# Softmax weights turned through VectorE and HBM in the attention and convolution layers of an encoder trunk

## The reference

```python
# differential attention: two softmaxes per head, one weight matrix w
probs = jax.nn.softmax(logits, axis=-1)
w = (probs[:, 0] - lam * probs[:, 1]).astype(v.dtype)
return jnp.einsum('bhqk,bkhe->bqhe', w, v)

# memory attention, in every layer
logits = jnp.einsum('bshd,bmhd->bhsm', q, km)
probs = jax.nn.softmax(logits, axis=-1)
return jnp.einsum('bhsm,bmhd->bshd', probs, vm)
```

## Time and profile before

| | |
|---|---|
| device time, median of 3 | 1245.73 us |
| span of the profiled execution, first to last instruction | 1244.68 us |
| what lies around the span, against the median | 1.05 us |
| PE busy | 1235.2 us, 99% |
| DVE busy | 1024.4 us, 82% |
| ACT busy | 730.3 us, 59% |
| mean granted TensorE clock | 0.998 |
| DMA queue of SP | 228.02 MB, 55.5% of 16 engines |

### The profile page before, as it was taken

How to read it: one execution, slowest core, us unless ns; L and a number is a source line. 1 busy time by engine, 2 the same in 40 slices (tenths; PEclk the granted TensorE clock), 3 DMA queues, 4 the chain that set the end, 5 groups by cost and what they waited for, 6 DMA issues and landing times.

```text
span 1244.7 us, 19689 instructions
## 1 busy us (share of the span) xinstructions
PE 1235.2 (99%) x7370; PEld 1082.9 (87%) x7370; DVE 1024.4 (82%) x1599; ACT 730.3 (59%) x1190; POOL 20.1 (2%) x29
## 2 busy tenths in 40 slices
PE   9999999999999999999999999999999999999997
PEld 7988888888999988888889888888888888888886
DVE  5876888889779888988887978988888776988887
ACT  6675765555766546555555546655554774755552
POOL 0001000000000100000000000000000001000000
PEclk9999999999999999999999999999999999999999
DMA  9834576554553345655655764656554533666651
GB/s 333 285 120 136 190 248 190 186 192 163 175 182 119 122 150 169 227 187 195 201 173 168 233 204 162 227 195 199 190 186 169 187 119 119 218 207 201 196 190 54
DMA packets 64539, 229.27 MB, mean 184 GB/s; under 512 B 7575, under 2 KB 9239, under 8 KB 63421
## 3 DMA queue, kind: packets, MB, share of 16 engines
q1 hardware_dynamic: 64444, 228.02, 55.5%
HBM read 226.93 MB, written 1.06 MB: 183 GB/s over the span
## 4 chain that ended last, share of the span: by engine, by line
PE 97%; DMA 1%; SPq 1%; DVE 0%; issue 0%; ACT 0%; DVEq 0%
PE pair L768 28%; PE acc L862 21%; PE pair L771 14%; PE pair L800 4%; PE pair L801 4%; PE pair L802 4%; PE acc L768 2%; PE acc L843 2%; PE acc L842 2%; PE acc L841 2%; PE pair L1022 2%; DMA raw<-in_stream 1%; PE pair L825 1%; PE pair L827 1%; PE pair L829 1%; PE acc L931 1%
## 5 line engine op out<-in xcount | busy, mean ns | idle before, releaser
L1278 DVE TENSOR_TENSOR w_lo<-raw,w_hi 128x1024 fp32r<-128x1024 f32 x400 | 482.6, 1221 | 105.3 <-ACT w_hi L1040 103.7
L1040 ACT ACTIVATE w_hi<-raw 128x1024 fp32r<-128x1024 f32 x400 | 420.5, 1058 | 213.2 <-PE pair L771 70.8
L768 PE MATMUL pair<-xT,w_hi 128*128 128x512 f32 x1520 | 477.8, 396 | 0.0
L771 PEld LDWEIGHTS pair<-xT,w_lo 128*128 128x128 f32 x1520 | 285.5, 188 | 67.2
L771 PE MATMUL pair<-xT,w_lo 128*128 128x256 f32 x1520 | 298.6, 278 | 0.0
L768 PEld LDWEIGHTS pair<-xT,w_hi 128*128 128x128 f32 x1520 | 233.8, 189 | 3.2 <-issue 0.3
L1087 ACT ACTIVATE hid<-pair 128x512 f32<-128x512 f32 x88 | 52.6, 597 | 124.9 <-PE pair L771 124.9
L1319 DVE TENSOR_TENSOR hid<-pair,hid 128x512 f32<-128x512 f32 x88 | 60.7, 690 | 47.9 <-ACT hid L1087 47.7
L800 PE MATMUL pair<-xT,w_hi 128*128 128x256 f32 x336 | 97.8, 291 | 0.0
L801 PE MATMUL pair<-xT,w_hi 128*128 128x256 f32 x336 | 95.0, 283 | 0.0
L802 PE MATMUL pair<-xT,w_lo 128*128 128x256 f32 x336 | 94.9, 283 | 0.0
(11 more groups left out here) (223 smaller groups left out, 1661.9 us busy)
## 6 DMA issues: line engine op xcount, KB each, us to landing
raw<-in_stream SPq DMA_DIRECT2D x400, 512.0 KB, 4.6
gains<-in_ln SPq DMA_DIRECT2D x8, 1024.0 KB, 8.4
bias<-bias_scratch SPq DMA_DIRECT2D x2, 1152.0 KB, 9.0
raw<-in_stream SPq DMA_DIRECT2D x8, 256.0 KB, 6.6
x_tok<-in_x_t SPq DMA_DIRECT2D x4, 256.0 KB, 6.2
y_tok<-in_mem_t SPq DMA_DIRECT2D x2, 512.0 KB, 7.1
x_tok<-in_x SPq DMA_DIRECT2D x1, 1024.0 KB, 6.5
out<-x_tok SPq DMA_DIRECT2D x4, 256.0 KB, 2.0
```

Of the source, the lines that this page charges most:

```text
L768: pe.matmul(bank, w_hi[:, slot, kk * P:(kk + 1) * P], xT[:, kk].rearrange("p a s -> p (a s)"), start=(kk == 0), stop=(kk == KT - 1), skip_ ...
L771: last = pe.matmul(bank[:, 0:SEQ], w_lo[:, slot, kk * P:(kk + 1) * P], xT[:, kk, 0, :], start=False, stop=(kk == KT - 1), skip_group_check ...
L1040: nc.scalar.activation(w_hi[:, u % SPLIT, :], raw[:, u % RAW, :], ACT.Copy).then_inc(hi_ready, 1)
L1278: v.tensor_tensor(w_lo[:, u % SPLIT, :], raw[:, u % RAW, :], w_hi[:, u % SPLIT, :].bitcast(F32), ALU.subtract).then_inc(lo_ready, 1)
```

## The change

- `xturn` stays in layer 1 alone. In layers 0, 2 and 3 it is replaced by `xswap` and `xfetch`; `turnw` of heads 0 to 3 in layers 0 and 3 by `swap`, `fetch` and `spread`. Heads 4 and 5 keep `turnw`.
- `xswap` and `swap` run on DVE right behind `xprob` and `prob`: one instruction that transposes 32x32 blocks, from `prob` into `ex` (128x1024) or within `prob` (128x512). It waits for DVE's own last instruction (`link`).
- For the same item SP waits for that instruction, then issues four stores of 32 partitions each into a scratch in HBM. `xfetch` and `fetch` wait on SP until all four have landed, then issue one load with 128 rows that brings the blocks into their place: 512 KB in runs of 1 KB for `xswap`, 256 KB in runs of 512 B for `swap`.
- For the memory heads PE reads the fetched tile directly, in runs of 32 elements. For heads 0 to 3 ACT puts it in order first (`spread`), one copy of 128x512 in place of the one from PSUM.
- SP now walks the item list too, so the loads of units stand between the swaps in its queue.
- Slots: the memory `xpv` move from 7 and 9 to 9 and 11 (attention), from 5 and 9 to 9 and 11 (convolution). `pv` 0 and 1 move from 13 to 14, `ms` 0, `tok` 0 and `scale` 0 by one. `xprob` 0 of the convolution layer moves from slot 1 to slot 0.

```diff
             at = {0: [it("xlog", 0), it("xlog", 1)], ...
-                  6: [it("exp", 0), it("xturn", 0)], 7: [it("exp", 1), it("xpv", 0)],
-                  8: [it("prob", 0), it("xturn", 1)], 9: [it("prob", 1), it("xpv", 1), it("log", 2), it("log", 3), it("turnw", 0)],
...
+                  2: [it("xexp", 1), it("xprob", 0), it("xswap", 0), it("xfetch", 0)],
+                  3: [it("xprob", 1), it("xswap", 1), it("xfetch", 1)],
+                  8: [it("prob", 0), it("swap", 0), it("fetch", 0)],
+                  9: [it("prob", 1), it("swap", 1), it("fetch", 1), it("xpv", 0), it("log", 2), it("log", 3)],
...
@@ sync @@
+                elif name in ("xswap", "swap"):
+                    n = weights_of(item)
+                    sp.wait_ge(swapped, swap_ord[n])
+                    for a in range(4):
+                        rows = slice(32 * a, 32 * a + 32)
+                        sp.dma_start(swap_scratch[n][a].rearrange("b i e -> i b e"), swap_source(n)[rows].rearrange(
+                            "i (b e) -> i b e", b=4)).then_inc(swap_stored[n % 2], 16)
+                elif name in ("xfetch", "fetch"):
+                    n = weights_of(item)
...
+                    if name == "fetch" and item[2] >= 2:
+                        sp.wait_ge(probT_ready, HEADS * (item[1] // 3) + item[2] - 1)
...
+                    sp.wait_ge(swap_stored[n % 2], 64 * swap_count[n])
+                    sp.dma_start(swap_target(n), swap_scratch[n].rearrange("a b i e -> (b i) a e")).then_inc(swap_landed[n % 2], 16)
@@ vector @@
+                elif name in ("xswap", "swap"):
+                    n = weights_of(item)
+                    of = prob[:, n % 2] if name == "xswap" else prob[:, n % 2, 0:1]
+                    v.transpose(swap_source(n).rearrange("p (b c j) -> p c b j", b=4, j=32),
+                                of.rearrange("p i t (k b j) -> p (i t k) b j", k=2, j=32)).then_inc(swapped, 1)
@@ scalar @@
+                elif name == "spread":
+                    n = prob_ord["", item[1], item[2]]
+                    act.wait_ge(swap_landed[n % 2], 16 * swap_count[n])
+                    nc.scalar.activation(probT[:, item[2]].rearrange("p t k (a j) -> p (t k) a j", a=4),
+                                         swap_target(n).rearrange("p a (c j) -> p c a j", j=32), ACT.Copy).then_inc(probT_ready, 1)
@@ tensor, xpv @@
+                    if n in swap_count:
+                        pe.wait_ge(swap_landed[n % 2], 16 * swap_count[n])
+                        weights = swap_target(n).rearrange("p a (i t k j) -> p i k t a j", i=2, t=2, k=2)
```

More of the change, by code:

```diff
@@ L364, in trunk_kernel @@
             prob = here("prob", [P, 2, 2, 2, SEQ])
-            xprobT = here("xprobT", [P, 2, 2, SEQ])
+            xprobT = here("xprobT", [P, 4 * SEQ])
         with ExitStack() as place:
@@ L502, in trunk_kernel @@
         scratch = nc.dram_tensor("bias_scratch", [HEADS, 512], F32, kind="Internal").ap()
+        swap_scratch = [nc.dram_tensor(f"swap_scratch{n}", [4, 4, 32, 256 if items[pos][0] == "xprob" else 128], F32, kind="Internal").ap()
+                        for n, pos in enumerate(prob_pos)]
         out_dram = out.rearrange("b (t p) d -> p (b t) d", p=P)
@@ L577, in x_count, with ex_free, swap_source, swap_target @@
             return 2 * (TT * m + t) + h + 1
+        def ex_free(n):
+            if n in swap_count:
+                return swap_stored[n % 2], 64 * swap_count[n]
+            return xprob_ready, items[prob_pos[n]][2] + 1
+        def swap_source(n):
+            s = n % 2
+            return (ex[:, s] if items[prob_pos[n]][0] == "xprob" else prob[:, s, 1:2]).rearrange("p i t s -> p (i t s)")
+        def swap_target(n):
+            name, layer, h = items[prob_pos[n]]
+            if name == "prob":
+                place = a_sq[:, 1 + h % 2]
+            elif h:
+                place = xprobT[:]
+            elif layer_kind(layer) == "attn":
+                place = probT[:, 4:6].rearrange("p h t k s -> p (h t k s)")
+            else:
+                place = prob[:, 0].rearrange("p i t s -> p (i t s)")
+            return place.rearrange("p (a e) -> p a e", a=4)
         def side_bank(pos, k=0):
@@ L619, in load_bias, with next_unit @@
                                               ap=[[1, P], [512, HEADS], [1, 384]])).then_inc(bias_landed, 16)
-            for u in range(RAW, 2 * nchunks):
+            def next_unit(u):
+                if u >= 2 * nchunks:
+                    return
                 c = u // 2
@@ L948, in _ @@
                 elif name == "turnw":
-                    n = prob_ord[pos]
+                    layer, h = item[1:]
+                    n = prob_ord["", layer, h]
+                    if ordinal[pos] == 0:
+                        pe.wait_ge(ident_landed, 16)
                     pe.wait_ge(prob_ready, ordinal[pos] + 1)
```

139 lines of the change are left out of this document (88 added, 51 removed).

## The result

The changed kernel takes 1247.67 us (median; 1246.58 to 1250.41) beside 1245.80 us for the kernel before on the same chip: ratio 1.0015, 95% interval 1.0008 to 1.0021. Forecast was 1239.7 us. The traced execution took 1246.73 us with a span of 1244.9, 0.2 us more span than before. The rest of the 1.9 us is scatter: the traced execution is one of the changed kernel's faster ones, and the one traced before was slower than its median. Every execution for which the record has both numbers took 1.7 to 2.0 us more than its span, so the 1244.68 us of span before belong to about 1246.5 us (an estimate). The 1.05 us in the table of the time before compare two different executions.

A forecast was written before the change was run, and what follows sets the result against it. PE, busy for 99% of the span, was taken as the bound. 8.05 us removed, less 0.15, 0.9 and 1.0, gave 6.0 us saved: 1239.7 us. Its own range was 1238 to 1242.5 us; with two rivals 1237.4 to 1245.5.

The forecast's parts named there:

- What leaves PE: Transposes removed from PE in layers 0, 2 and 3: six memory groups and heads 0 to 3, 8.05 us together.
- The products stay, only their places move: On PE, the products remain as work and only change slots; no instruction is added.
- The term of 1.0 us for waits in the attention layers: PE waiting 0.5 us in each of two attention layers for the HBM path, bounds 0 and 4.0 us.
- Strided reads: Memory product on PE reading runs of 32 elements: 24 matmuls, 0.15 us added.
- the wait at CG 2: Convolution layer: PE arrives early and waits for `prod_ready`, handing back 0.9 us of the layer's 1.59 us.
- The room of "over a microsecond": Convolution layer, two chunks after CG 2: the next `prod_ready` wait has over a microsecond of slack.
- Block transposes: On DVE, six large at 1.22 us and eight small at 0.61 us; 13.6 us of DVE time with waits.
- rival B: DVE block transposes take two passes, 2.45 us; gain 0.7 us, 1245.0 us, no change; chance 0.17.
- The trip: Heads' weights through HBM before `pv` in attention layers: 3.0 us per landing, 9 us against 11.8 us of room.
- rival C: HBM round trip sets the time of `pv`: 6.2 us per landing, 13.6 us late, 1252.3 us; chance 0.13.
- The weight stream: SP's unit loads queue behind stores and fetches; holds of some 5 us, costed at nothing.
- my cover: Ring of weight units nearly always full, 5 units or some 14 us ahead, taken to cover SP's holds.

The follow-up runs named there:

- e13: The whole change in the slots of the kernel before, without the HBM trip in the attention layers (output not the reference's): 1239.78 us.
- e3: The changed kernel with the convolution layer's memory attention as in the kernel before: 1247.67 us.
- e4: The changed kernel without DVE's block transposes, stores and fetches kept (output not the reference's): 1246.64 us.
- e6: The changed kernel without the HBM trip in the attention layers, block transposes kept (output not the reference's): 1247.03 us.
- e9: Kernel before with only memory attention of layers 0, 2 and 3 through DVE and HBM, `xpv` in the old slots: 1241.68 us.
- e11: The whole change, HBM trip included, in the slots of the kernel before: 1247.07 us.
- e2: The changed kernel with `ms` 0 and `tok` 0 one slot earlier: 1246.35 us.
- e5: e2 with ACT's order changed, second seed and `scale` 0's `mixT_hi` ahead of spreads: 1245.97 us.
- e12: e9 plus heads 2 and 3 through DVE and HBM; heads 0 and 1 on TensorE, old slots: 1240.76 us.
- e7: Kernel before with only the attention layers' memory attention through DVE and HBM, `xpv` 0 and 1 in slots 8 and 9: 1251.73 us.

## Why the prediction was wrong

- *What leaves PE* (8.05 us) was right as work, if anything low: where nothing else moves, the offset steps by 0.88 us for a pair (0.79 forecast) and by 0.35 to 0.5 for a head. That e13 ends at nearly the forecast's 1239.7 us is chance: it too loses some 2 us, but at other places than the forecast has them (1.1 at `pv` 0, 0.5 and 0.4 at `scale` 0).
- *"The products stay, only their places move"* is the step that failed. I costed a moved `pv` by what it frees on PE and asked only whether its inputs are there. I didn't follow its outputs: `ms`, `tok` and `scale` 0 moved along, behind other instructions of ACT and DVE. The term of 1.0 us for waits in the attention layers measured 2.5 + 0.6 in layer 0 and 2.3 + 1.6 in layer 3, 7.0 us. The row for it was there before: `tok` ended at 90.14, and `scale` ran at 90.25, so any move of that chain behind PE shows at once.
- *The clock* has no term in the prediction at all. 1.6 of those 7.0 us are not waiting but work at a granted clock of 0.50 behind the wait. The scatter of the slower kernels goes with it: e3 has two such stretches of 3.4 us (from 92.7 and from 1024.6), e4 one in layer 3, e6 one in layer 0, though the waits at `scale` 0 are alike in all of them.
- *Strided reads* were forecast at 0.15 us and cost nothing: a matmul of the memory product took 379 ns (median) before and after. There are 48 of them by the trace's count, not 24.
- *Convolution:* the wait at CG 2 was forecast at 0.9 and measured at 0.85. The room of "over a microsecond" was told for the next `prod_ready`; what came instead is another wait, 0.61 us of `xpv` 1 in slot 11 for the side bank. And the wait at CG 2 exists only because `xpv` 0 was moved from in front of it (e9).
- *Block transposes* were sized well:
```profile
L1651 DVE STREAM_TRANSPOSE ex<-prob 128x1024 f32<-128x1024 f32 x6 | 7.5, 1245 | 0.2
L1651 DVE STREAM_TRANSPOSE prob<-prob 128x512 f32<-128x512 f32 x8 | 5.7, 712 | 0.3
```
  1.22 and 0.61 were forecast; rival B (two passes) is out. (Its sum has a slip: the 1.1 us are 3.97 less 2.9, and the 1.22 beside them are the second pair's.) By the medians e4, without them, is 1.0 us faster.
- *The trip:* forecast to be ready at 76.7, measured at 79.7, the `spread` included. In this trace PE didn't wait for it, with 0.1 us to spare; in e3's and e4's it waited 1.8 us in layer 0. So rival C came about only in part. Its mechanism, the trip that sets the time of `pv`, is real: the move of `pv` from 13 to 14 paid for most of it in advance, and e13 against e11 prices it at 7.3 us in the old slots, the clock included.
- *The weight stream:* my cover was too thin. ACT waited 25.7 us for landed units (8.0 before, at most 2.6 at a time),
```profile
ACT w_hi L1119 <- DMA raw<-in_stream: 25.7, 24, 6.5
```
  and PE 0.2 us for `w_lo`. The longest of ACT's waits lies in the convolution layer and reaches PE by a detour: DVE's `w_lo` comes late behind it, and the `mixT_lo` for which `xpv` 1 waits stands behind that `w_lo`. Over the kernels with the same slots there the two go together: ACT waits 6.1, 6.3, 6.5, 7.0 and 7.9 us (e2, e5, the change, e6, e4), PE at `xpv` 1 not at all, 0.3, 0.6, 1.0 and 1.4.

The same prices fit e12: its turns are worth 8.05 less 2 x 0.76 for heads 0 and 1, so 6.5 us; 0.4 go back at a memory product of layer 0 and 0.45 at `scale` 0 of each attention layer, and 5.2 are left beside 5.1 measured. The Trainium skill ("VectorE: DVE Perf Modes", rules for kernel authors) puts a 128x128 transpose on TensorE where a result in PSUM will do. Here TensorE bounds, and e12 moves ten of the fourteen tiles off it with gain, 1240.76 us against 1245.88, so the measurement goes against the rule; the change with its moved slots didn't gain. Open: why the clock falls behind a wait of 2.3 us in one place and not behind one of 2.5 in another, and so what share of each median it has; and why head 0's stores take from 7.8 to 10.6 us to let its fetch go (the change, e4). Neither was tried.

## What to carry to other kernels

In a hand-ordered kernel, price a moved step by both its ends: what it waits for, and every in-order queue that its results pass through afterwards, down to where the bounding engine meets them. Ask first whether the same work can leave the bounding engine without moving a slot; here that part gave 5 us, and the moved slots alone cost 8, the clock included. Look at the granted clock behind every new wait of TensorE: the wait can cost more than it shows. A trip through memory suits those tiles whose consumer stands several slots away (memory heads, heads 2 and 3), not those on the short chain.

## What the runs showed of the hardware

A wait of TensorE can cost about twice its length. In e11 PE stood 3.1 us, the granted clock was 0.50 for 6.8 us from within that wait on, and 3.4 us more were lost; in e7 two waits of 3.3 and 2.2 us were each followed by 3.4 us at 0.50, 1.7 us lost each; in the changed kernel a wait of 2.3 us was, and one of 2.5 was not. In each case PE had been at work again when the clock came back to 1.00.

Small stores cost the issuing queue more than their size says. A head's 256 KB go out as four stores of 64 KB: in layer 0 SP issued them in 1.9 us, and over all heads it then stood for their landing 3.9 us on average (31.0 us over 8 waits) and up to 5.9, with units of 512 KB issued shortly ahead. From head 0's first store to the issue of its fetch it was 7.8 us in layer 0, where a 256 KB store in the quiet end of the kernel landed in 2.0. Behind such holds ACT waited up to 6.5 us for a unit, though SP had mostly waited for a free slot of the ring before.
